# The first loads and splits in smaller pieces: quarters of weights, eighths of x on ScalarE's queue

## The reference

```python
def rmsnorm(x, g):
    xf = x.astype(jnp.float32)
    y = xf * lax.rsqrt(jnp.mean(xf * xf, axis=-1, keepdims=True) + EPS)
    return (y * g.astype(jnp.float32)).astype(x.dtype)

def hybrid_layer(x, g_mix, w_in, ...):
    h = rmsnorm(x, g_mix) @ w_in
    z, xbc, dt, q, k, v, qi, ki, wi = _split(h, IN_SIZES)
    ...
```

## Time and profile before

| | |
|---|---|
| median of three executions | 2676.37 us (2675.97 to 2680.64) |
| the profiled execution's span | 2674.5 us |
| TensorE busy | 2637.4 us (99%) |
| VectorE busy | 1741.5 us (65%) |
| ScalarE busy | 1325.8 us (50%) |
| GpSimd busy | 208.4 us (8%) |
| read from HBM | 473.29 MB |
| mean rate of all loads and stores | 180 GB/s |

### The profile page before, as it was taken

How to read it: one execution, slowest core, us unless ns; L and a number is a source line. 1 busy time by engine, 2 the same in 40 slices (tenths; PEclk the granted TensorE clock), 3 DMA queues, 4 the chain that set the end, 5 groups by cost and what they waited for, 6 DMA issues and landing times. The chain is left out here.

```text
span 2674.5 us, 35946 instructions
## 1 busy us (share of the span) xinstructions
PE 2637.4 (99%) x14484; PEld 2270.5 (85%) x14484; DVE 1741.5 (65%) x2361; ACT 1325.8 (50%) x1903; POOL 208.4 (8%) x182
## 2 busy tenths in 40 slices
PE   9999999999999999999999999999999999999998
PEld 8778888888888888888889888988888888888886
DVE  7788797555556555695776767566665455565554
ACT  6545455535445344465554545455455354453443
POOL 3014001000000000140411300000000000000000
PEclk9999999999999999999999999999999999999999
DMA  7644445555555555566333333354555555555553
GB/s 267 164 170 151 166 173 186 193 189 189 190 188 189 205 175 202 178 251 252 142 129 139 126 127 120 132 205 175 198 196 189 190 188 193 185 189 205 179 199 126
DMA packets 68173, 481.91 MB, mean 180 GB/s; under 512 B 8007, under 2 KB 8135, under 8 KB 11176
## 3 DMA queue, kind: packets, MB, share of 16 engines
q1 hardware_dynamic: 65088, 466.65, 49.1%
q0 software_dynamic: 1968, 10.75, 1.5%
q10 hardware_dynamic: 952, 2.22, 0.2%
HBM read 473.29 MB, written 6.29 MB: 179 GB/s over the span
## 5 line engine op out<-in xcount | busy, mean ns | idle before, releaser
L1253 DVE TENSOR_TENSOR w_lo<-weight_ring,w_hi 128x1024 fp32r<-128x1024 f32 x882 | 1083.7, 1239 | 695.0 <-ACT w_hi L2104 694.0
L2104 ACT CAST w_hi<-weight_ring 128x1024 fp32r<-128x1024 f32 x884 | 919.8, 1052 | 640.9 <-PE bank L545 407.4
L533 PE MATMUL bank<-h,w_hi 128*128 128x512 f32 x2848 | 905.3, 399 | 0.0
L536 PEld LDWEIGHTS bank<-h,w_lo 128*128 128x128 f32 x2848 | 535.0, 188 | 126.2
L533 PE MATMUL bank<-mix,w_hi 128*128 128x512 f32 x1776 | 568.0, 401 | 4.1 <-DVE w_lo L1253 1.9
L536 PE MATMUL bank<-h,w_lo 128*128 128x256 f32 x2848 | 560.1, 278 | 0.0
L533 PEld LDWEIGHTS bank<-h,w_hi 128*128 128x128 f32 x2848 | 436.3, 189 | 7.6 <-issue 5.8
L543 PE MATMUL bank<-w_hi,mix 128*128 128x512 f32 x1056 | 411.2, 389 | 0.0
L544 PE MATMUL bank<-w_lo,mix 128*128 128x512 f32 x1056 | 410.9, 389 | 0.0
L545 PE MATMUL bank<-w_hi,mix 128*128 128x512 f32 x1056 | 410.8, 389 | 0.0
L536 PEld LDWEIGHTS bank<-mix,w_lo 128*128 128x128 f32 x1776 | 333.8, 188 | 78.8
(11 more groups left out here) (369 smaller groups left out, 1761.0 us busy)
## 6 DMA issues: line engine op xcount, KB each, us to landing
weight_ring<-in_w_up SPq DMA_DIRECT2D x128, 1024.0 KB, 4.8
weight_ring<-in_w_down SPq DMA_DIRECT2D x128, 1024.0 KB, 4.8
weight_ring<-in_w_merge SPq DMA_DIRECT2D x32, 1024.0 KB, 4.8
weight_ring<-in_w_gdn SPq DMA_DIRECT2D x24, 1024.0 KB, 4.9
weight_ring<-in_w_papb SPq DMA_DIRECT2D x16, 1024.0 KB, 4.7
weight_ring<-in_w_o SPq DMA_DIRECT2D x16, 1024.0 KB, 4.8
weight_ring<-in_w_xbc SPq DMA_DIRECT2D x12, 1024.0 KB, 4.7
weight_ring<-in_w_q SPq DMA_DIRECT2D x8, 1024.0 KB, 4.8
```

Of the source, the lines that this page charges most:

```text
L533: e.matmul(bank[:, :], w_hi[:, unit_at % UNITS, o + j * P:o + (j + 1) * P], x[:, :, at + j * S:at + (j + 1) * S], start=first and j == 0, ...
L536: done = e.matmul(bank[:, 0:S], w_lo[:, unit_at % UNITS, o + j * P:o + (j + 1) * P], x[:, 0, at + j * S:at + (j + 1) * S], start=False, st ...
L1253: e.tensor_tensor(w_lo[:, i, :], ring[:, p % PIECES, half * UNIT:(half + 1) * UNIT], w_hi[:, i, :].bitcast(F32), ALU.subtract).then_inc(un ...
L2104: e.copy(w_hi[:, i, :], ring[:, p % PIECES, half * UNIT:(half + 1) * UNIT]).then_inc(unit_hi, 1)
```

## The change

SyncE's first four loads are now quarters of pieces (512 columns, 256 KB) in the order piece 0, piece 1, piece 0, piece 1; the second halves of pieces 0 and 1 follow directly, then piece 2. The loads of x are issued on ScalarE's queue, as eight parts of two k-tiles (256 KB), behind the load of `vecs` and before the tiny activation. ScalarE's and VectorE's `first_quarter(i)` split half a unit each, for units 0 and 1, between the x tiles: quarter 0, x tiles 0 and 1, quarter 1, x tiles 2 and 3, quarters 2 and 3, x tiles 4 to 7, then units 2 and 3 as before. TensorE's first column pair is `first_pair`, with the same products in the same order; for k-tiles 0 to 3 it waits for a new semaphore, `first_lo`, that counts the first two quarters, and for k-tiles 4 to 7 for `unit_lo`. Its waits for `unit_lo` are now also in front of each four k-tiles.

```diff
+            def first_pair(x, ready):
+                nonlocal unit, use
+                banks = []
+                for _ in range(2):
+                    banks.append(bank_free())
+                    use += 1
+                for k0 in range(0, KD, 4):
+                    for j in range(2):
+                        if k0 == 0:
+                            e.wait_ge(first_lo, j + 1)
+                        else:
+                            e.wait_ge(unit_lo, unit + 2 * (k0 // UNIT_K) + j + 1)
+                        for k in range(k0, k0 + 4):
+                            if j == 0 and k % 2 == 0:
+                                e.wait_ge(ready[0], ready[1][k])
+                            n = unit + 2 * (k // UNIT_K) + j
+                            done = products(banks[j], n, (k % UNIT_K) * P, P, x, k * S, k == 0, k == KD - 1)
+                            if k % UNIT_K == UNIT_K - 1:
+                                done.then_inc(unit_used, 1)
+                unit += 4
...
-            column_pair(mix, gained_x(0), 4)
+            first_pair(mix, gained_x(0))
...
+            def first_quarter(i):
+
+                nonlocal made
+                at = slice(i // 2 * (UNIT // 2), (i // 2 + 1) * (UNIT // 2))
+                if i < 2:
+                    e.wait_ge(first_hi, i + 1)
+                else:
+                    e.wait_ge(unit_hi, made + 1)
+                done = e.tensor_tensor(w_lo[:, i % 2, at], ring[:, i % 2, at], w_hi[:, i % 2, at].bitcast(F32), ALU.subtract)
+                if i < 2:
+                    done.then_inc(first_lo, 1)
+                else:
+                    done.then_inc(unit_lo, 1)
+                    made += 1
+
             e.wait_ge(ones_set, 3)
-            split_to(1)
+            first_quarter(0)
             e.wait_ge(vecs_loaded, 16)
             for t in range(KD):
-                if t % 4 == 0:
-                    e.wait_ge(x_loaded[t // 4], 16)
+                if t % 2 == 0:
+                    e.wait_ge(x_loaded[t // 2], 16)
                 gained(t, "g_mix", mix)
-                if t % 4 == 3 and t < 8:
-                    split_to(t // 2 + 1)
+                if t == 1:
+                    first_quarter(1)
+                elif t == 3:
+                    first_quarter(2)
+                    first_quarter(3)
+                elif t == 7:
+                    split_to(4)
             column_pair(qiT)
...
             e.dma_start(vecs[:, :], t_in["vecs"]).then_inc(vecs_loaded, 16)
+            for n in range(8):
+                part = slice(n * 2 * S, (n + 1) * 2 * S)
+                e.dma_start(xT[:, part], t_in["x"][:, part]).then_inc(x_loaded[n], 16)
             e.wait_ge(ones_set, 3)
 
             e.activation(root_1[:, 0:1], ones[:, 0:1], ACT.Copy, scale=1.0)
-            e.wait_ge(first_loaded[0], 16)
-            split_to(1)
+            def first_quarter(i):
+
+                nonlocal made
+                at = slice(i // 2 * (UNIT // 2), (i // 2 + 1) * (UNIT // 2))
+                e.wait_ge(first_loaded[i], 16)
+                done = e.copy(w_hi[:, i % 2, at], ring[:, i % 2, at])
+                if i < 2:
+                    done.then_inc(first_hi, 1)
+                else:
+                    done.then_inc(unit_hi, 1)
+                    made += 1
+
+            first_quarter(0)
             e.wait_ge(vecs_loaded, 16)
             for t in range(KD):
-                if t % 4 == 0:
-                    e.wait_ge(x_loaded[t // 4], 16)
+                if t % 2 == 0:
+                    e.wait_ge(x_loaded[t // 2], 16)
                 e.activation(tile(mix_hi, t), tile(xT, t), ACT.Copy, scale=vec("g_mix", t)).then_inc(xg_hi, 1)
-                if t == 3:
-                    e.wait_ge(first_loaded[1], 16)
-                    split_to(2)
+                if t == 1:
+                    first_quarter(1)
+                elif t == 3:
+                    first_quarter(2)
+                    first_quarter(3)
                 elif t == 7:
                     split_to(4)
...
-            e.dma_start(ring[:, 0, 0:UNIT], order[0][:, 0:UNIT]).then_inc(first_loaded[0], 16)
-            load_x(0)
-            e.dma_start(ring[:, 1, 0:UNIT], order[1][:, 0:UNIT]).then_inc(first_loaded[1], 16)
-            load_x(1)
+            for i in range(4):
+                at = slice(i // 2 * (UNIT // 2), (i // 2 + 1) * (UNIT // 2))
+                e.dma_start(ring[:, i % 2, at], order[i % 2][:, at]).then_inc(first_loaded[i], 16)
             for n in range(2):
                 e.dma_start(ring[:, n, UNIT:PIECE], order[n][:, UNIT:PIECE]).then_inc(piece_loaded[n], 16)
-            load_x(2)
-            load_x(3)
```

More of the change, by code:

```diff
@@ L461, in build @@
         vecs_loaded, params_loaded = sem("vecs_loaded"), sem("params_loaded")
-        x_loaded = [sem(f"x_loaded{i}") for i in range(4)]
-        first_loaded = [sem(f"first_half_loaded{i}") for i in range(2)]
+        x_loaded = [sem(f"x_loaded{i}") for i in range(8)]
+        first_loaded = [sem(f"first_quarter_loaded{i}") for i in range(4)]
+        first_hi, first_lo = sem("first_quarters_hi"), sem("first_quarters_lo")
         piece_loaded = [sem(f"piece_loaded{i}") for i in range(PIECES)]
@@ L2869, in _ @@
         def _(e):
-            def load_x(n):
-                part = slice(n * KD * S // 4, (n + 1) * KD * S // 4)
-                e.dma_start(xT[:, part], t_in["x"][:, part]).then_inc(x_loaded[n], 16)
-            e.dma_start(ring[:, 0, 0:UNIT], order[0][:, 0:UNIT]).then_inc(first_loaded[0], 16)
-            load_x(0)
-            e.dma_start(ring[:, 1, 0:UNIT], order[1][:, 0:UNIT]).then_inc(first_loaded[1], 16)
-            load_x(1)
+            for i in range(4):
+                at = slice(i // 2 * (UNIT // 2), (i // 2 + 1) * (UNIT // 2))
+                e.dma_start(ring[:, i % 2, at], order[i % 2][:, at]).then_inc(first_loaded[i], 16)
             for n in range(2):
                 e.dma_start(ring[:, n, UNIT:PIECE], order[n][:, UNIT:PIECE]).then_inc(piece_loaded[n], 16)
-            load_x(2)
-            load_x(3)
             for n, piece in enumerate(order):
```

## The result

The changed kernel takes 2683.94 us (median of 8 executions), the kernel before 2677.28 in the same comparison (8): a ratio of 1.0024, 95% interval 1.0015 to 1.0032. It is slower, by 6.7 us, and outside the predicted range.

The account below looks back on a forecast made before the run. TensorE itself was taken to bound the opening after its start; ScalarE's issues start it 0.49 us later, ending the column pair about 0.3 late: span 2674.5 + 0.3 = 2674.8 us, median 2676.7, range 2673.8 to 2680.6.

Parts of the forecast that it names:

- The bound: First 23 us: TensorE itself bounds the stretch after 9.21 us; before it, loads, casts and differences hold its start.
- The issues on ScalarE: Opening: eight x issues at 0.59 us each delay the table load to 5.90 us and free ScalarE at 7.40.
- the two queues share the engines equally: Opening loads: assumed equal bytes per queue, landing weight quarter 0 near 5.4 us and x eighth 0 at 6.6.
- k-tile 8: First column pair: tile 9 ready at 17.77 us, wanted at 17.83; just no wait, with unit 3 landing at 14.6.
- my sum: Opening: ScalarE from 7.40 us, TensorE starts at 9.70, 0.49 later; column pair ends about 0.3 us late.
- For that stretch the second rule is not borne out: Opening loads: doubted the skill's advice of 1 MiB transfers, since 512 KB loads already moved 442 GB/s in 14 to 15 us.
- second rival: Opening loads: smaller rows keep 333 GB/s, TensorE waits about 1.8 us before k-tile 8; 2678.5 us; chance 0.17.
- fourth rival: First column pair: stops between k-tiles keep the clock at 1.2 GHz, 0.29 us more per pair; up to 2683.1; chance 0.04.
- first and third rivals: Opening: cheap issues, early second halves, 2675.8 or 2674.3 us, chance 0.22; or k-tile 8 takes back the gain, 2676.4, 0.15.
- the cap by a late tile: First column pair: with tile 9 at 17.8 us, the end is 23.35 at the soonest, whatever the start.

Follow-up runs that it names:

- the run with 2 KB rows: Changed kernel with SyncE's second halves and pieces 2 and 3 issued as 256 KB loads with 2 KB rows; median 2680.71 us, ratio 1.0014.
- the pieces were held: Changed kernel with SyncE issuing piece 2 and what follows only after the last x eighth landed; median 2679.30 us, ratio 1.0010.
- one queue: Changed kernel with its eight x loads moved from ScalarE's queue to SyncE's, between the weight loads; median 2677.24 us, ratio 0.9999 to before.
- order: Kernel with all small loads on SyncE's queue, plus x eighths 4 and 5 loaded and split ahead of unit 3; median 2678.03 us, ratio 0.9997.
- queue alone: Kernel before with only its four x quarters (4 KB rows) issued on ScalarE's queue; median 2678.84 us, ratio 1.0007.

## Why the prediction was wrong, point by point

**The bound.** Right: the opening decides. 7.5 of 7.9 us lie there.

**The issues on ScalarE.** Right in kind, a little small in size: I took 0.59 us an issue and a table load at 5.90; eight took 5.24, 0.66 each, near the upper bound of 0.67 (SyncE's longest in the trace before was in fact 0.69), and the table load began at 6.45. The start came at 10.19, not 9.70. That is 0.5 us of the error. The size varies: eight such issues took 0.59 each in the run with 2 KB rows (its start, 9.65, is my 9.70) and 0.71 where the pieces were held.

**The step that failed: "the two queues share the engines equally".** I wrote that the trace before could not test it. It could. There vecs, with rows of 1.4 KB on ScalarE's queue, loads beside SyncE's 4 KB rows. The view by queue of the kernel before, 2 to 5 us:

```profile
q1 hardware_dynamic: 159, 0.60, 66.6%
q10 hardware_dynamic: 135, 0.17, 27.5%
```

159 and 135 packets, 0.60 and 0.17 MB: nearly equal turns, far from equal bytes.

The Trainium skill has the rule, in DMA: Bandwidth & Descriptors, under Queues, rings and completion order: each engine goes round between the queue rows that have work, a packet at a time. The packet counts of 198 and 199 agree. The page gives 9 to 17 descriptors as typical of a packet; what takes turns in this trace are the single rows, by the constant difference shown with the result. I had weighed another section of that page and not this one.

With turns by packet the sum comes out near what happened. By my rule of equal shares, which I did not write out this far, tiles 14 and 15 were to be there when 2 x (2.10 + 0.18) + 0.4 = 4.96 MB had moved, near 15.6 us; they came at 25.60. Beside 8 KB rows, at a fifth of some 425 GB/s, an eighth of 0.26 MB takes 3.1 us (an estimate from the view of 13 to 16 us), and the last four eighths landed at 16.4, 19.6, 22.5 and 25.6.

On the whole x did better than that at the end, and it didn't help. From 18 us on, with pieces 2 and 3 nearly moved, it took 0.37 of 0.80 MB (18 to 20 us, first fence), and only 0.08 of its 2.10 MB were left for the five us that follow (second fence). By then pieces 4 and 5, issued at 16.8 and 18.0, moved with their 8 KB rows.

```profile
q1 hardware_dynamic: 67, 0.43, 55.1%
q10 hardware_dynamic: 209, 0.37, 49.1%
```

```profile
q1 hardware_dynamic: 260, 1.90, 91.3%
q10 hardware_dynamic: 48, 0.08, 4.3%
```

A load has landed only when its last row has, so the 3.1 us is the pace of the rows that are furthest behind. It would fit if a few of the 16 engines never ran out of weights; the trace doesn't show by engine, and this part stays open.

I stopped at k-tile 8. There two errors of mine cancelled, which is luck: unit 3 landed at 14.5 us (issued at 3.16, 11.3 to landing), where I had said 14.6, because its queue got more than half of a stream that was slower than before (329 GB/s against 408 in 8 to 11 us). It was cast at about 15.5 since ScalarE had stood 0.98 us for x tile 6, TensorE went on with k-tile 8 at 18.87 against 17.8 in my sum, and the waits came at k-tiles 10, 12 and 14, where I had looked no further.

**"For that stretch the second rule is not borne out"** (small loads). Neither confirmed nor refuted by these runs, since row size and number of queues both go with the rate early on and matter little later. From 6 to 9 us one queue moved 0.98 and 1.01 MB with 2 KB rows (one queue, first row; order) and 1.05 to 1.11 with 4 KB rows (the three profiles of before); two queues moved 1.02 with 2 KB rows (the run with 2 KB rows on both) and 1.24 with 4 KB rows (queue alone, last two rows).

```profile
q1 hardware_dynamic: 538, 0.98, 96.4%
```

```profile
q10 hardware_dynamic: 170, 0.63, 52.3%
q1 hardware_dynamic: 165, 0.61, 49.7%
```

From 13 to 16 us the run with 2 KB rows alone, on both queues, moved 1.19 MB, 397 GB/s, and from 16 to 19 us, nearly all on one queue, 389 GB/s. So 2 KB rows are not bound to some 330 GB/s. My second rival had about the right rate (333 GB/s) and the consequence wrong: the rate lasted to about 11 us, in 13 to 16 us the changed kernel moved 1.28 MB, and the one-queue kernel, with the same small loads, ended its pair no later than before.

**The fourth rival, the clock.** Its mechanism occurred, as a follower. TensorE stood still for 2.09 us before 27.15, the granted clock in 27 to 30 us was 0.51, and four pairs took 0.68 each. Price 1.3 us, not 5.4. In the second profile of the changed kernel the granted clock was 1.00 in 26 to 30 us; there the pair after an earlier stop, at 21.13, is a slow one, and the end is 29.98. The clock follows the waits and adds to them; it isn't their cause.

**The first and third rivals** asked for an earlier start. With the table load first it came (8.26), and the pair ended at 30.09 all the same; the cap by a late tile is what I had described, only two to six k-tiles further on.

**The chances.** I gave slower by over 0.2% 0.05, and all of that to the clock and to the spread of the runs. The assumption of equal shares, on which the landings of the sum rested, had no rival of its own that starves x; had it been one, its price would have been about 6 us (an estimate from these rows: with the last eighth at 25.60, k-tile 14 started at 27.15, and it was wanted at 15.13 + 17 x 0.347 = 21.0).

## What to carry to other kernels

What a second DMA queue changes first is who gets the bytes: between two busy queues they go by the row sizes of their loads. It added little bandwidth here (1.24 against 1.05 to 1.11 MB in 6 to 9 us with 4 KB rows, nothing in 13 to 16 us: 1.27 and 1.28 against 1.29). Keep what is wanted first in one queue in the order of need, or give the urgent loads rows as large as those they run beside, and check what comes late instead (with x in 8 KB rows it was the first weights); above all don't let prefetches with large rows run next to urgent small ones. Before moving a load, read packets and MB by queue in a stretch where two queues are busy, and follow every k-tile to the end of the stage, not only the first that looks tight. None of the variants beat the kernel before by an amount that its median shows.

## What the runs showed of the hardware that I had not expected

- Turns by packet, one row each, over row pairs of 2 KB and 8 KB (145 and 144 packets), 4 and 4 (172, 173), 4 and 8 (113, 111), 8 and 2 (142, 136).
- A load's landing followed its slowest rows: 0.08 of x's 2.10 MB were left at 20 us, and the last eighth landed at 25.6.
- In 6 to 9 us, 2 KB rows on one queue moved 328 GB/s and 4 KB rows on two queues 414 GB/s; in 13 to 16 us 2 KB rows on two queues moved 397.
- An issue on ScalarE's queue took 0.59 to 0.71 us on average with two queues busy and eight in a row, and 0.42 us when it was the first (vecs).
- Three executions of one unchanged kernel differed by 3.5 us in span, 1.8 of it by how long the clock was low in the first 24 us.
